# Two first weight sums by accumulating DMA, and a fifth row block pair in seven products, in a two-block transformer kernel

## The chip, the cores and the metric

The kernel runs on one core of one Trainium2 chip. The metric is the device time of one execution in microseconds; the time before is the median of three runs. [...]

## The reference

Two blocks of a transformer, each of two layers, run one after the other on 256 tokens of width 2048, in float32. The change touches one product: the gates of the two layers of the second block (layers 2 and 3 in the kernel's count).

```python
def hybrid_layer(x, norm_w, w_in, ...):
    h = rms_norm_2(x, norm_w)
    proj = h @ w_in                     # (256 x 2048) @ (2048 x 17808)
    (qa, ka, va, za, qi, ki, wi, ub, zb, qc, kc, vc, zc, gates) = jnp.split(proj, ...)
    y_a = (dsa_attention(...) * jax.nn.silu(za)) @ w_a_out
    y_b = (conformer_conv(...) * jax.nn.silu(zb)) @ w_b_out
    y_c = (stick_breaking_attention(...) * jax.nn.silu(zc)) @ w_c_out
    g = jax.nn.sigmoid(gates).reshape(b, s, N_BRANCH, D_MODEL)
    merged = g[:, :, 0] * y_a + g[:, :, 1] * y_b + g[:, :, 2] * y_c
    return x + merged @ w_out
```

The gates are 6144 columns wide: three branches of 2048.

## The kernel before

**Streaming of weights.** Each weight matrix passes once, in fills. A fill is 256 rows of a weight by 512 columns (512 KB), loaded by a DMA that SP issues into one of six buffers `raw`. ACT rounds it to `wh` (step `hi`), DVE computes the rest `wl = raw - wh` (step `lo`), each into one of five buffers (`SPLIT = 5`), and PE multiplies: a product of a 128 x 128 block of the input with a 128 x 512 block of the weight is three matmuls of 512 columns (`wh` with the input's high part, `wl` with the high part, `wh` with its low part). The input has 256 tokens, so 2 blocks of rows, and a fill has 2 blocks of weight rows: 4 products for each fill.

**Seven products for eight.** Two neighbouring gate gemms, a (left 512 columns) and b (right 512 columns), form a duo. A duo has eight row block pairs (256 rows of the weight each), so in the plain way two fills and 8 products for each pair. A pair with a star in the strings `GATES_OF_2` and `GATES_OF_3` is done by the Strassen-Winograd scheme in 7 products, in four fills: `a` (2 products), `b` (2), `x` (2) and `y` (1). With the blocks B11, B21 of a and B12, B22 of b, the sums of weight blocks were: `t_outer`, x = (B12 - B11, B12 - B22), one DVE instruction of 1024 columns into a third buffer; `t_inner`, B22 - x[0]; `t_last`, B21 minus that, 512 columns each. `hi` and `lo` then run on x and y too. The matching sums of the input (`s_sum`, `s_hi`, `s_lo`) are made once in a layer for each starred pair number and serve all gate duos. The products go to six PSUM banks, which `duo_copy`, `duo_middle`, `duo_outer`, `duo_inner` and `duo_end` join. Each layer has five gate duos of this kind (`GATES`), with starred pairs 1, 2, 4, 6; a duo is followed by the two gemms y (1024 rows by 512 columns each) that it gates.

**Buffers of x.** In the gates x has three places beside the six `raw` (`place_raw`): two are made of four of the five `tmp` buffers, one lies in a region of `G`. They are used in turn, and one is free again once `lo` of its x fill is done.

**Order.** All engines run in order. The order is made ahead of time by a planner (`Plan.settle`): it plays all steps through with an estimated duration and gives each engine the step that can start first. The order of pairs in a duo is the string's order. `raw` is issued as soon as its buffer's last reader (`lo`) is done. The gate duos of layer 2 lie at about 1548 to 1850 us, those of layer 3 at 2554 to 2855 us.

Of the kernel before, what the change touches and what calls it, by code (L numbers as in the profile page):

```python
# [12 lines left out]
RAW = 6  # L13
# [3 lines left out]
XS = 3  # L17
# [102 lines left out]
class Lane:  # L120
# [118 lines left out]
    def dma_add(self, dst, src):  # L239
        if self.e is None:  # L240
            self.plan.step.dma = size(dst) * dst.shape[0] * 4
            self.plan.step.late = 2500.0
            return self.sketch(900)
        return self.e.dma_start(dst, src, accum_op=ALU.add)
# [22 lines left out]
class Plan:  # L267
# [16 lines left out]
    def settle(self, urgency):  # L284
# [21 lines left out]
        while self.done < total:  # L306
# [113 lines left out]
class Program:  # L420
# [426 lines left out]
    def sums_at(self, key, q):  # L847

        kind, L = key
        i = SUMS.get(f"{kind}{L}", SUMS.get(kind)).index(q)  # L850
        if kind == "h":
            hi, lo = self.pairs["Y"][L]
            at = (16, 14)[L] + 2 * i
            hi, lo = (x[:, at:at + 2, :].rearrange("p a b -> p (a b)") for x in (hi, lo))
        elif kind == "mem":
            hi, lo = (x[:, 16 + 2 * i:18 + 2 * i, :].rearrange("p a b -> p (a b)") for x in self.pairs["Y"][0])
        elif kind == "out" and L < 2:
            hi, lo = (self.R[:, 1, 1024 * i + 512 * x:1024 * i + 512 * x + 512] for x in range(2))
        elif kind == "out":
            hi, lo = self.pairs["Y"][L]  # L860
            hi, lo = (x[:, 8 + 2 * i:10 + 2 * i, :].rearrange("p a b -> p (a b)") for x in (hi, lo))
        elif key == ("ub", 2) and i == 2 or kind == "gate" and i == 3:
            hi, lo = self.R[:, 0, 4096:4608], self.R[:, 1, 4096:4608]
        elif kind == "gate" and i > 3:
            hi, lo = (self.R[:, 5 - i, 512 * x:512 * x + 512] for x in range(2))
# [5 lines left out]
    def free_sums(self, key):  # L871

        kind, L = key
        if kind == "gate":
            gid = {2: 12, 3: 16}[L]
            return [*self.y_moved(gid),
                    self.v_zb.at(*((L - 2, c) for c in range(0, 8, 2))),
                    *self.y_moved(gid - 1)]
        if kind == "mem":
            return []  # L880
        if key in (("out", 0), ("out", 1)):
            return [self.v_in.at((("y", 3, 2), ("y", 8, 0))[L])]
        if kind == "out":
# [60 lines left out]
    def spare(self, of, c):  # L944
# [277 lines left out]


def sp_program(P, e):
    def load_memt(n):
# [39 lines left out]

    return {"load_memt": load_memt, "load_mem2": load_mem2, "raw": raw, "store": store, "stored": stored}


def pool_program(P, e):
# [297 lines left out]
def act_program(P, e):  # L1567
# [23 lines left out]
    def hi(f):  # L1591
# [5 lines left out]
        role = P.role[f][0] if f in P.role else None  # L1597
        if role in ("b", "x", "y"):
            e.wait_ge(*P.v_tsum.at((f - "abxy".index(role), {"b": 2, "x": 1, "y": 4}[role])))
        if role not in ("x", "y"):  # L1600
# [18 lines left out]
    def s_hi(of, q):  # L1619
        s = P.tmp.buf(("S", of, q)).rearrange("p (n c) -> p n c", n=4)  # L1620
        e.wait_ge(*P.v_ssum.at(*((of, q, i) for i in range(1, 5))))
        for w in P.free_sums(of):
            e.wait_ge(*w)
# [397 lines left out]
def dve_program(P, e):  # L2021
# [18 lines left out]
    def t_outer(f):  # L2040

        a, b, x = (P.slot[f + i] for i in range(3))
        L = P.fills[f][0].L
        if x >= RAW and P.beside[L, x - RAW][0] == f + 2:
            if x == RAW + 2:
                for w in P.y_moved(13 + 4 * (L - 2)):
                    e.wait_ge(*w)
            else:
                for i in range(2 * (x - RAW), 2 * (x - RAW) + 2):
                    P.tmp.take(("beside", L, i), i)  # L2050
                    e.wait_ge(*P.tmp.free(("beside", L, i)))
        e.wait_ge(*P.raw_loaded(f))
        e.wait_ge(*P.raw_loaded(f + 1))
        if P.leaves[f + 2] is not None:
            e.wait_ge(*P.v_lo.at(P.leaves[f + 2]))
        i, j = 2 * a, 2 * b + 1
        s = slice(i, j + 1, j - i) if i < j else slice(i, j - 1 if j else None, j - i)
        b12 = P.raw[b][:, 0, :].unsqueeze(1).broadcast_to([128, 2, 512])
        e.tensor_tensor(P.raw[x], b12, P.raws[:, s, :], ALU.subtract).then_inc(*P.v_tsum.up((f, 1)))

    def t_inner(f):
        a, b, x = (P.raw[P.slot[f + i]] for i in range(3))
        e.wait_ge(*P.v_tsum.at((f, 1)))
        e.tensor_tensor(b[:, 0, :], b[:, 1, :], x[:, 0, :], ALU.subtract).then_inc(*P.v_tsum.up((f, 2)))

    def t_last(f):
        a, b = (P.raw[P.slot[f + i]] for i in range(2))
        e.wait_ge(*P.v_tsum.at((f, 2)))
        e.wait_ge(*P.v_lo.at(f))
        e.tensor_tensor(a[:, 1, :], a[:, 1, :], b[:, 0, :], ALU.subtract).then_inc(*P.v_tsum.up((f, 4)))  # L2070

    def s_sum(of, q):
# [15 lines left out]
        e.wait_ge(*P.v_ssum.at((*key, "a")))  # L2088
        e.tensor_tensor(s[:, 0, :], a[:, 0, 128:256], a[:, 1, 128:256], ALU.add).then_inc(*P.v_ssum.up((*key, 1)))
        e.tensor_tensor(s[:, 1, :], a[:, 0, 128:256], a[:, 0, 0:128], ALU.subtract).then_inc(*P.v_ssum.up((*key, 3)))  # L2090
        e.wait_ge(*P.v_ssum.at((*key, 1)))
        e.tensor_tensor(s[:, 2, :], s[:, 0, :], a[:, 0, 0:128], ALU.subtract).then_inc(*P.v_ssum.up((*key, 2)))
        e.wait_ge(*P.v_ssum.at((*key, 2)))
# [10 lines left out]
    def duo_middle(n):  # L2104
# [21 lines left out]
    def duo_end(g):  # L2126
# [202 lines left out]
    def flip_x(of, c):  # L2329
# [456 lines left out]
def add_steps(P):  # L2786
# [254 lines left out]
    for f, (gm, _) in enumerate(P.fills):  # L3041
# [152 lines left out]
```

## Time and profile before

| | before |
|---|---|
| median of 3 runs | 2986.84 us (2985.16 to 2987.07) |
| the profiled execution, its own time | 2987.06 us |
| its span | 2985.3 us |
| PE busy | 2967.4 us, 99% |
| PE weight load busy | 2479.1 us, 83% |
| DVE busy | 2525.8 us, 85% |
| ACT busy | 2242.2 us, 75% |
| POOL busy | 8.3 us |
| DMA | 570.34 MB, mean 191 GB/s |

The chain of waits gives PE 96% of the span. A matmul of 512 columns is listed with some 388 ns, but these lie over one another, so the listed durations of a group add up to more than the time they take; the time of a matmul on the path is the distance between the starts of two in a row.

### The profile page before, as it was taken

What the parts mean: (1) busy time and instruction counts of PE and PEld (TensorE: products, weight loads), DVE (VectorE), ACT (ScalarE), POOL (GpSimd) and SP (SyncE); (2) the same over time, 40 slices, a digit from 0 to 9 for tenths busy, and PEclk for the clock granted to TensorE, in tenths of its full rate; (3) what the DMA queues carried; (4) which work ended last, traced back from release to release, by engine and by line L of the source; (5) the groups of instructions that cost most, each with busy time, mean ns of one, the idle gap of its engine ahead of it and who ended that gap; (6) DMA issues with size and microseconds to landing.
All of it is one profiled execution on the core that took longest, in us unless ns stands there. A gap on an engine that the chain in (4) does not pass through costs nothing.

```text
span 2985.3 us, 38308 instructions
## 1 busy us (share of the span) xinstructions
PE 2967.4 (99%) x13679; PEld 2479.1 (83%) x13679; DVE 2525.8 (85%) x4023; ACT 2242.2 (75%) x3827; POOL 8.3 (0%) x21
## 2 busy tenths in 40 slices
PE   8999999999999999999999999999999999999998
PEld 7888888877888888888888888888888888888887
DVE  6778679787779899999988888888998998888887
ACT  8797686968877676799885557677778999665684
POOL 0000000000000000000000000000000000000000
PEclk9999999999999999999999999999999999999999
DMA  9656656665556575556565666666565666566565
GB/s 328 191 166 178 179 165 218 205 181 173 177 171 216 170 220 170 177 170 190 177 194 181 202 208 204 205 198 197 154 195 176 182 185 183 177 213 204 181 205 176
DMA packets 305838, 570.34 MB, mean 191 GB/s; under 512 B 18368, under 2 KB 45152, under 8 KB 305264
## 3 DMA queue, kind: packets, MB, share of 16 engines
q1 hardware_dynamic: 301728, 557.65, 59.8%
q10 hardware_dynamic: 3040, 6.42, 0.6%
q0 software_dynamic: 880, 3.83, 0.4%
q8 instruction: 108, 1.77, 0.2%
q14 instruction: 82, 0.67, 0.1%
HBM read 565.73 MB, written 2.10 MB: 190 GB/s over the span
## 4 chain that ended last, share of the span: by engine, by line
PE 96%; DVE 1%; ACT 1%; DMA 1%; issue 0%; DVEq 0%; SPq 0%; ACTq 0%
PE gp L152 83%; PE bk L152 13%; ACT G L167 1%; DVE wl L178 1%; ACT wh L167 0%; DMA raw<-in_w_in 0%; DMA raw<-in_ev_w_mem_kv 0%; DVE merged L231 0%; PE bk L155 0%; DVE merged L178 0%; DVE nat L184 0%; DVE nat L178 0%; DVE merged L184 0%; DVE raw L178 0%; DVE merged L191 0%
## 5 line engine op out<-in xcount | busy, mean ns | idle before, releaser
L167 ACT ACTIVATE wh<-raw 128x1024 fp32r<-128x1024 f32 (+2 forms) x1138 | 1148.6, 1024 | 580.6 <-PE gp L152 459.8
L178 DVE TENSOR_TENSOR wl<-raw,wh 128x1024 fp32r<-128x1024 f32 (+2 forms) x1138 | 1319.5, 1174 | 296.7 <-ACT wh L167 289.7
L152 PE MATMUL gp<-wh,Hh 128*128 128x512 f32 (+3 forms) x2130 | 825.6, 388 | 0.6 <-DVE wl L178 0.5
L152 PE MATMUL gp<-wl,Hh 128*128 128x512 f32 (+3 forms) x2130 | 818.2, 384 | 0.0
L152 PE MATMUL gp<-wh,Hl 128*128 128x512 f32 (+3 forms) x2130 | 818.0, 384 | 0.0
L152 PE MATMUL gp<-wh,Yh 128*128 128x512 f32 (+2 forms) x1676 | 651.3, 389 | 9.2 <-DVE wl L178 9.2
L152 PE MATMUL gp<-wh,Yl 128*128 128x512 f32 (+2 forms) x1676 | 646.6, 386 | 0.0
L152 PE MATMUL gp<-wl,Yh 128*128 128x512 f32 (+2 forms) x1676 | 646.6, 386 | 0.0
L152 PEld LDWEIGHTS gp<-wh,Hh 128*128 128x128 f32 x2130 | 400.2, 188 | 80.7 <-issue 2.2
L152 PEld LDWEIGHTS gp<-wh,Hl 128*128 128x128 f32 x2130 | 400.1, 188 | 78.7
L152 PEld LDWEIGHTS gp<-wl,Hh 128*128 128x128 f32 x2130 | 400.2, 188 | 76.7
L152 PEld LDWEIGHTS gp<-wh,Yh 128*128 128x128 f32 x1676 | 315.5, 188 | 71.8 <-DVE wl L178 10.1
L152 PEld LDWEIGHTS gp<-wh,Yl 128*128 128x128 f32 x1676 | 315.4, 188 | 62.2
L152 PEld LDWEIGHTS gp<-wl,Yh 128*128 128x128 f32 x1676 | 315.6, 188 | 61.1
L167 ACT ACTIVATE G<-nat 32x256 f32<-32x256 f32 (+2 forms) x672 | 264.9, 394 | 11.3 <-DVE nat L231 1.9
L184 DVE SCALAR_TENSOR_TENSOR merged<-merged,cc 128x256 f32<-128x256 f32 x480 | 201.4, 478 | 0.0
L167 ACT ACTIVATE G<-tmp 32x192 f32<-32x192 f32 (+1 forms) x416 | 153.6, 369 | 6.7 <-DVE tmp L231 1.0
L167 ACT ACTIVATE nat<-gp,small 128x512 f32<-128x512 f32 (+3 forms) x178 | 102.6, 621 | 52.3 <-PE gp L152 49.8
L167 ACT ACTIVATE G<-G 32x256 f32<-32x256 f32 (+1 forms) x284 | 117.2, 413 | 4.3 <-DVE G L231 0.3
L152 PE MATMUL bk<-G 128*128 128x128 f32 (+5 forms) x796 | 117.3, 308 | 0.0
L152 PEld LDWEIGHTS bk<-G 128*128 128x128 f32 (+2 forms) x796 | 100.2, 186 | 12.6 <-issue 4.4
L152 PE MATMUL bk<-wh,R 128*128 128x512 f32 x294 | 106.5, 389 | 0.0
(177 smaller groups left out, 2375.9 us busy)
## 6 DMA issues: line engine op xcount, KB each, us to landing
raw<-in_w_in SPq DMA_DIRECT2D x544, 512.0 KB, 4.2
raw<-in_ev_w_in SPq DMA_DIRECT2D x104, 512.0 KB, 4.3
raw<-in_od_w_in SPq DMA_DIRECT2D x80, 512.0 KB, 4.0
raw<-in_w_out SPq DMA_DIRECT2D x64, 512.0 KB, 5.2
raw<-in_ev_w_out SPq DMA_DIRECT2D x40, 512.0 KB, 4.4
raw<-in_od_w_out SPq DMA_DIRECT2D x36, 512.0 KB, 4.6
raw<-in_w_b_out SPq DMA_DIRECT2D x32, 512.0 KB, 4.9
raw<-in_w_a_out SPq DMA_DIRECT2D x32, 512.0 KB, 5.0
```

Source lines behind the costliest of these rows:

```text
L152: return self.e.matmul(out, l, r, start=start, stop=stop)
L167: return self.e.activation(out, in_, func, **kw)
L178: return self.sketch(157 + size(a) * 1.042) if self.e is None else self.e.tensor_tensor(out, a, b, op)
L184: return self.e.scalar_tensor_tensor(out=out, in0=a, scalar=s, in1=b, op0=op0, op1=op1)
```

## The change

Pair 5 gets a star in all ten gate duos of layers 2 and 3 (`GATES_OF_2`, `GATES_OF_3`): five of eight pairs in 7 products. Of the five starred pairs of a duo the second to the fifth in its order (`NTH_BY_DMA`) no longer have `t_outer` on DVE: SP loads B11 and B22 once more, into the two halves of x (`blocks`, two DMAs of 256 KB), and POOL issues two accumulating DMAs that add B12 from HBM to each half (`blocks_add`). For this all sums change their signs: x = (B12 + B11, B12 + B22), and so on, and the signs in `s_sum`, `duo_middle`, `duo_end` and `duo_residual` change with them; the count of instructions there does not. `t_inner` and `hi` of x wait for the accumulating DMAs. `blocks` may be issued five fills ahead (`AHEAD`), waits for its place to be free, in SP's queue, and at its first use for the sums of the input.

Further: `BY_DMA = ((0, 1),)` gives the adding of one of four `merge` steps of branch 0 to two accumulating DMAs on POOL, in each layer. Sums of the input in `out` of layers 0 and 1 lie in another buffer, so two waits (`load_mem2`, `flip_x`) go. The planner's estimate of DMA time changes (400 to 360 bytes a nanosecond, an accumulating one 1.63 times its size), so that it may order steps otherwise anywhere.

```diff
-BY_DMA = ()
+NTH_BY_DMA = (1, 2, 3, 4)
+AHEAD = 5
+BLOCKS_BY_DMA = (("gate", 2), ("gate", 3))
+BY_DMA = ((0, 1),)
...
-GATES_OF_2 = ('0 *1 3 *2 *4 5 *6 7', '0a *1 *2 3b 0b 3a 5 *6 *4 7', ...
+GATES_OF_2 = ('0 *1 3 *2 *4 *5 *6 7', '0a *1 *2 3b 0b 3a *5 *6 *4 7', ...
...
+    def added_up(self, f):
+        d = self.role[f][1]
+        nth = [u for u in d.units if self.role[u][0] == "a"].index(f)
+        return d.sums in BLOCKS_BY_DMA and nth in NTH_BY_DMA and self.slot[f + 2] >= RAW
...
+    def blocks(f):
+
+        (a, j), b, x = P.fills[f], P.fills[f + 1][0], P.slot[f + 2]
+        e.behind("raw", P.loaded_before[f + 1 - AHEAD])
+        room_beside(P, e, f)
+        for h, gm in enumerate((a, b)):
+            k, c = 256 * j + 128 * h, gm.ranges[0][0]
+            e.dma_start(P.raw[x][:, h, :], gm.w[k:k + 128, c:c + 512]).then_inc(*P.s_xload[x - RAW].up((f, h), 16))
...
+    def blocks_add(f):
+
+        b, j = P.fills[f + 1]
+        x, c = P.slot[f + 2], b.ranges[0][0]
+        e.wait_ge(*P.s_xload[x - RAW].at((f, 0), (f, 1)))
+        for h in range(2):
+            e.dma_add(P.raw[x][:, h, :], b.w[256 * j:256 * j + 128, c:c + 512]).then_inc(*P.s_xadd[x - RAW][h].up(f, 16))
...
-        e.tensor_tensor(P.raw[x], b12, P.raws[:, s, :], ALU.subtract).then_inc(*P.v_tsum.up((f, 1)))
+        e.tensor_tensor(P.raw[x], b12, P.raws[:, s, :], ALU.add).then_inc(*P.v_tsum.up((f, 1)))
 
     def t_inner(f):
         a, b, x = (P.raw[P.slot[f + i]] for i in range(3))
-        e.wait_ge(*P.v_tsum.at((f, 1)))
-        e.tensor_tensor(b[:, 0, :], b[:, 1, :], x[:, 0, :], ALU.subtract).then_inc(*P.v_tsum.up((f, 2)))
+        for w in P.first_sums(f, 0):
+            e.wait_ge(*w)
+        if P.added_up(f):
+            e.wait_ge(*P.raw_loaded(f + 1))
+        e.tensor_tensor(b[:, 0, :], b[:, 1, :], x[:, 0, :], ALU.add).then_inc(*P.v_tsum.up((f, 2)))
...
         if role == "a":
-            for s in ("t_outer", "t_inner", "t_last"):
+            if P.added_up(f):
+                add("sp", "blocks", f)
+                add("pool", "blocks_add", f)
+            else:
+                add("dve", "t_outer", f)
+            for s in ("t_inner", "t_last"):
                 add("dve", s, f)
```

How the order moves. SP's queue in layer 2, from the last loads ahead of the first gate duo on. Before:

```order
L237 DMA raw<-in_w_b_out 128x2x512 x4
L237 DMA raw<-in_w_in 128x2x512 x16
L237 DMA raw<-in_w_b_out 128x2x512 x8
L237 DMA raw<-in_w_in 128x2x512 x16
L237 DMA raw<-in_w_a_out 128x2x512 x8
```

The same place now, where `tmp` and `G` are the places of x:

```order
L240 DMA raw<-in_w_b_out 128x2x512 x4
L240 DMA raw<-in_w_in 128x2x512 x6
L240 DMA tmp<-in_w_in 128x512 x2
L240 DMA G<-in_w_in 128x512 x2
L240 DMA raw<-in_w_in 128x2x512 x2
L240 DMA tmp<-in_w_in 128x512 x2
L240 DMA raw<-in_w_in 128x2x512 x4
L240 DMA tmp<-in_w_in 128x512 x2
L240 DMA raw<-in_w_in 128x2x512 x4
L240 DMA raw<-in_w_b_out 128x2x512 x8
```

Between the 16 fills of the first gate duo now stand four pairs of half-size loads. POOL, which had nothing in the gates but constants, gets this there (layer 2, first 22 accumulating DMAs):

```order
L230 MEMSET merged 128x8x30
L247 DMA tmp<-in_w_in 128x512 x2
L247 DMA G<-in_w_in 128x512 x2
L247 DMA tmp<-in_w_in 128x512 x8
L247 DMA G<-in_w_in 128x512 x2
L247 DMA tmp<-in_w_in 128x512 x2
L247 DMA G<-in_w_in 128x512 x2
L247 DMA tmp<-in_w_in 128x512 x2
L247 DMA merged<-nat 128x512 x2
```

Each row of two is one starred pair; the row on `merged` is the merge step. DVE in the first gate duo of layer 2, before:

```order
L178 TENSOR_TENSOR wl3<-raw,wh3 128x1024
L178 TENSOR_TENSOR G<-raw 128x1024
L178 TENSOR_TENSOR wl4<-raw,wh4 128x1024
L178 TENSOR_TENSOR wl0<-raw,wh0 128x1024
L178 TENSOR_TENSOR raw<-raw 128x512
L178 TENSOR_TENSOR wl1<-tmp,wh1 128x1024
L178 TENSOR_TENSOR raw<-raw,G 128x512
L178 TENSOR_TENSOR wl2<-raw,wh2 128x512
```

and now:

```order
L181 TENSOR_TENSOR wl3<-raw,wh3 128x1024
L181 TENSOR_TENSOR raw<-raw,G 128x512
L181 TENSOR_TENSOR wl4<-raw,wh4 128x1024
L181 TENSOR_TENSOR wl0<-raw,wh0 128x1024
L181 TENSOR_TENSOR raw<-raw 128x512
L181 TENSOR_TENSOR wl1<-tmp,wh1 128x1024
L181 TENSOR_TENSOR wl2<-raw,wh2 128x512
L181 TENSOR_TENSOR raw<-raw,tmp 128x512
```

`G<-raw` (`t_outer`) is gone, and `raw<-raw,G` (`t_inner`) stands in its place; it now waits for a DMA, in front of the next `lo`.

## Rows read from the trace of the kernel before

**Rows 1.** The page: span, and busy time of each engine.
```profile
span 2985.3 us, 38308 instructions
PE 2967.4 (99%) x13679; PEld 2479.1 (83%) x13679; DVE 2525.8 (85%) x4023; ACT 2242.2 (75%) x3827; POOL 8.3 (0%) x21
```

**Rows 2.** The chain of waits: shares by engine; two long pieces (start, us, what).
```profile
PE 96%; DVE 1%; ACT 1%; DMA 1%; issue 0%; DVEq 0%; SPq 0%; ACTq 0%
...
918.39 48.96 PE bk L152 x216
...
1474.16 48.99 PE gp L152 x216
```

**Rows 3.** The waits of PE: total, times, longest, in us.
```profile
PE gp L152 <- DVE wl L178: 9.7, 4, 8.5
PE bk L152 <- DVE merged L178: 0.2, 1, 0.2
```

**Rows 4.** Timeline of PE, fifth gate duo of layer 2: start, duration, operation [idle before].
```profile
1836.67 0.39 PE L152 MATMUL bk<-wl,R 128*128 128x512 f32 x1
1836.89 0.39 PE L152 MATMUL bk<-wh,R 128*128 128x512 f32 x1
1837.38 0.50 PE L152 MATMUL gp<-wh,Hh 128*128 128x512 f32 x1
...
1837.96 0.40 PE L152 MATMUL gp<-wh,Hl 128*128 128x512 f32 x1
1838.86 0.50 PE L152 MATMUL gp<-wh,Hh 128*128 128x512 f32 x1 [0.51 <-DVE wl L178]
```

**Rows 5.** Windows in the gates: length, busy time of each engine, clock, DMA share, GB/s.
```profile
1618.00:1622.00 4.00, 4.00 (x19) 3.32 (x18) 2.31 (x2) 1.24 (x2) 0.00 (x0) 1.00 1.01 355
...
1646.00:1650.00 4.00, 4.00 (x19) 3.30 (x19) 3.59 (x4) 2.97 (x3) 0.00 (x0) 1.00 1.03 378
1595.00:1850.00 255.00, 254.40 (x1121) 210.00 (x1121) 220.80 (x218) 155.06 (x185) 0.00 (x0) 1.00 0.62 202
```

**Rows 6.** DVE from 1595 to 1850 us, by form: count, busy, mean ns, idle before.
```profile
L178 DVE TENSOR_TENSOR wl<-raw,wh 128x1024 fp32r<-128x1024 f32 x98 | 118.0, 1220 | 19.8 <-ACT wh L167 18.7
L178 DVE TENSOR_TENSOR tmp<-raw 128x1024 f32<-128x1024 f32 x12 | 14.7, 1223 | 5.5 <-DMA raw<-in_w_in 5.4
...
L178 DVE TENSOR_TENSOR raw<-raw 128x512 f32<-128x512 f32 x16 | 11.0, 687 | 0.4
L178 DVE TENSOR_TENSOR wl<-raw,wh 128x512 fp32r<-128x512 f32 x15 | 10.3, 686 | 2.4 <-ACT wh L167 2.4
...
L178 DVE TENSOR_TENSOR merged<-nat,merged 128x1024 f32<-128x1024 f32 x6 | 7.4, 1226 | 0.2
```

**Rows 7.** ACT in the same stretch, by form.
```profile
L167 ACT ACTIVATE wh<-raw 128x1024 fp32r<-128x1024 f32 x97 | 101.6, 1058 | 73.7 <-PE gp L152 58.3 <-DVE raw L178 12.8 <-PE bk L152 1.7
...
L167 ACT ACTIVATE wh<-raw 128x512 fp32r<-128x512 f32 x16 | 10.1, 629 | 12.1 <-PE gp L152 8.3 <-DVE raw L178 2.7 <-PE bk L152 1.1
```

**Rows 8.** Waits in the same stretch, all engines: total, times, longest.
```profile
ACT wh L167 <- PE gp L152: 73.3, 66, 2.1
...
DVE tmp L178 <- DMA raw<-in_w_in: 5.4, 6, 1.5
```

**Rows 9.** DMA issues: count, KB each, median us from issue to landing.
```profile
raw<-in_ev_w_mem_kv SPq DMA_DIRECT2D x16, 512.0 KB, 8.6
...
raw<-in_w_in SPq DMA_DIRECT2D x32, 256.0 KB, 3.2
...
tab<-in_c_tab POOLq DMA_DIRECT2D x2, 256.0 KB, 4.0
```

**Rows 10.** DMA issues of 1595 to 1850 us alone.
```profile
raw<-in_w_in SPq DMA_DIRECT2D x65, 512.0 KB, 4.8
```

**Rows 11.** Waits of SP's queue over the whole span.
```profile
SPq L237 <- DVE wl L178: 2500.5, 991, 12.2
```

More of the change, by code:

```diff
@@ L241, in dma_add @@
             self.plan.step.dma = size(dst) * dst.shape[0] * 4
-            self.plan.step.late = 2500.0
+            self.plan.step.late, self.plan.step.dma = 2500.0, self.plan.step.dma * 1.63
             return self.sketch(900)
@@ L496, in signals @@
         self.s_raw = [sig(f"s_raw{i}") for i in range(RAW)]
+        self.s_xload = [sig(f"s_xload{i}") for i in range(XS)]
+        self.s_xadd = [[sig(f"s_xadd{i}{h}") for h in range(2)] for i in range(XS)]
         self.s_mem = [sig(f"s_mem_{i}") for i in range(4)]
@@ L831, in by_dve, with first_sums @@
         return BY_DVE and gm.L < 2 and gm.g > 13 and f not in self.role and f % BY_DVE == 0
+    def added_up(self, f):
+        d = self.role[f][1]
+        nth = [u for u in d.units if self.role[u][0] == "a"].index(f)
+        return d.sums in BLOCKS_BY_DMA and nth in NTH_BY_DMA and self.slot[f + 2] >= RAW
+    def first_sums(self, f, *halves):
+        if self.added_up(f):
+            return [self.s_xadd[self.slot[f + 2] - RAW][h].at(f) for h in halves]
+        return [self.v_tsum.at((f, 1))]
     def raw_loaded(self, f):
@@ L857, in sums_at @@
         elif kind == "out" and L < 2:
-            hi, lo = (self.R[:, 1, 1024 * i + 512 * x:1024 * i + 512 * x + 512] for x in range(2))
+            hi, lo = (x[:, 8 + 2 * i:10 + 2 * i, :].rearrange("p a b -> p (a b)") for x in self.pairs["H"][L])
         elif kind == "out":
@@ L864, in sums_at @@
         elif kind == "gate" and i > 3:
-            hi, lo = (self.R[:, 5 - i, 512 * x:512 * x + 512] for x in range(2))
+            hi, lo = (self.R[:, 1, 2048 + 512 * x:2560 + 512 * x] for x in range(2))
         else:
@@ L869, in sums_at, with free_sums @@
         return tuple(x.rearrange("p (n c) -> p n c", n=4) for x in (hi, lo))
[L871 removed]
+    def free_sums(self, key, q):
         kind, L = key
@@ L875, in free_sums @@
             gid = {2: 12, 3: 16}[L]
-            return [*self.y_moved(gid),
+            return [*self.y_moved(gid), *(self.y_moved(gid + 1) if SUMS["gate"].index(q) > 3 else []),
                     self.v_zb.at(*((L - 2, c) for c in range(0, 8, 2))),
@@ L881, in free_sums @@
         if key in (("out", 0), ("out", 1)):
-            return [self.v_in.at((("y", 3, 2), ("y", 8, 0))[L])]
+            return [self.p_mm.at(self.h_end[L].end)]
         if kind == "out":
@@ L1221, in gated, with room_beside @@
         return r[:, :, gr.dh * h:gr.dh * h + gr.dh]
+def room_beside(P, e, f):
+    x, L, d = P.slot[f + 2], P.fills[f][0].L, P.role[f][1]
+    if x >= RAW and P.added_up(f):
+        e.wait_ge(*P.v_s.at(*((d.sums, q) for q in SUMS[d.sums[0]])))
+    if x >= RAW and P.beside[L, x - RAW][0] == f + 2:
+        if x == RAW + 2:
+            for w in P.y_moved(13 + 4 * (L - 2)):
+                e.wait_ge(*w)
+        else:
+            for i in range(2 * (x - RAW), 2 * (x - RAW) + 2):
+                P.tmp.take(("beside", L, i), i)
+                e.wait_ge(*P.tmp.free(("beside", L, i)))
+    if P.leaves[f + 2] is not None:
+        e.wait_ge(*P.v_lo.at(P.leaves[f + 2]))
 def sp_program(P, e):
@@ L1264, in stored @@
         e.wait_ge(*P.s_out[n].at("o"))
-    return {"load_memt": load_memt, "load_mem2": load_mem2, "raw": raw, "store": store, "stored": stored}
+    return {"load_memt": load_memt, "load_mem2": load_mem2, "raw": raw, "blocks": blocks, "store": store, "stored": stored}
 def pool_program(P, e):
@@ L1597, in hi @@
         role = P.role[f][0] if f in P.role else None
-        if role in ("b", "x", "y"):
-            e.wait_ge(*P.v_tsum.at((f - "abxy".index(role), {"b": 2, "x": 1, "y": 4}[role])))
+        if role == "x":
+            for w in P.first_sums(f - 2, 0, 1):
+                e.wait_ge(*w)
+        if role in ("b", "y"):
+            e.wait_ge(*P.v_tsum.at((f - "abxy".index(role), {"b": 2, "y": 4}[role])))
         if role not in ("x", "y"):
@@ L1621, in s_hi @@
         e.wait_ge(*P.v_ssum.at(*((of, q, i) for i in range(1, 5))))
-        for w in P.free_sums(of):
+        for w in P.free_sums(of, q):
             e.wait_ge(*w)
@@ L2042, in t_outer @@
         a, b, x = (P.slot[f + i] for i in range(3))
[L2043 to L2051, printed above, removed]
+        room_beside(P, e, f)
         e.wait_ge(*P.raw_loaded(f))
         e.wait_ge(*P.raw_loaded(f + 1))
-        if P.leaves[f + 2] is not None:
-            e.wait_ge(*P.v_lo.at(P.leaves[f + 2]))
         i, j = 2 * a, 2 * b + 1
@@ L2069, in t_last @@
         e.wait_ge(*P.v_lo.at(f))
-        e.tensor_tensor(a[:, 1, :], a[:, 1, :], b[:, 0, :], ALU.subtract).then_inc(*P.v_tsum.up((f, 4)))
+        e.tensor_tensor(a[:, 1, :], a[:, 1, :], b[:, 0, :], ALU.add).then_inc(*P.v_tsum.up((f, 4)))
     def s_sum(of, q):
@@ L2078, in s_sum @@
         e.wait_ge(*P.v_in.at(P.lhs(gm, 2 * q)))
-        for w in P.free_sums(of):
+        for w in P.free_sums(of, q):
             e.wait_ge(*w)
@@ L2088, in s_sum @@
         e.wait_ge(*P.v_ssum.at((*key, "a")))
[L2089 to L2090 removed]
+        e.tensor_tensor(s[:, 0, :], a[:, 1, 128:256], a[:, 0, 128:256], ALU.subtract).then_inc(*P.v_ssum.up((*key, 1)))
+        e.tensor_tensor(s[:, 1, :], a[:, 0, 0:128], a[:, 0, 128:256], ALU.subtract).then_inc(*P.v_ssum.up((*key, 3)))
         e.wait_ge(*P.v_ssum.at((*key, 1)))
[L2092 removed]
+        e.tensor_tensor(s[:, 2, :], s[:, 0, :], a[:, 0, 0:128], ALU.add).then_inc(*P.v_ssum.up((*key, 2)))
         e.wait_ge(*P.v_ssum.at((*key, 2)))
@@ L2108, in duo_middle @@
         e.wait_ge(*P.p_mm.at(d.last["6"][0]))
-        e.tensor_tensor(T[:, 3, :], P.banks_of(d)["6"], T[:, 0, :], ALU.add).then_inc(*v.up((n, "v1")))
+        e.tensor_tensor(T[:, 3, :], T[:, 0, :], P.banks_of(d)["6"], ALU.subtract).then_inc(*v.up((n, "v1")))
         P.bank.give(("duo", n, "6"), v, (n, "v1"))
@@ L2132, in duo_end @@
         b = P.nat.buf(g)
-        e.tensor_tensor(b, b, P.gp[g % 2][:, :, :], ALU.add).then_inc(*P.v_duo.up((n, "c" + x)))
+        e.tensor_tensor(b, P.gp[g % 2][:, :, :], b, ALU.add if x == "a" else ALU.subtract).then_inc(*P.v_duo.up((n, "c" + x)))
     def duo_residual(g):
@@ L2143, in duo_residual @@
         x = P.X[:, :, 512 * gm.part:512 * gm.part + 512]
-        e.tensor_tensor(x, P.nat.buf(g), x, ALU.add).then_inc(*P.v_duo.up((gm.duo.n, g)))
+        e.tensor_tensor(x, x, P.nat.buf(g), ALU.add if gm is gm.duo.a else ALU.subtract).then_inc(*P.v_duo.up((gm.duo.n, g)))
     def in_lo(of, i):
@@ L2340, in flip_x @@
             e.wait_ge(*P.p_mm.at(P.last_sums(("gate", 2))))
-        if of == ("x", 2) and P.outs[1][0].duo:
-            e.wait_ge(*P.p_mm.at(P.last_sums(("out", 1))))
         if c >= 2:
```

14 lines of the change are left out of this document (7 added, 7 removed).

## The prediction, on record before the changed kernel ran

> **What bounds the kernel now.** I read the page first: PE is busy 2967.4 of 2985.3 us [rows 1]. The chain of waits says the same, PE 96% [rows 2], and PE's own waits come to 9.9 us in the whole run, 8.5 of it a single one [rows 3]. So PE's instructions, not their supply, set the time, and the first question is what one matmul costs there. The groups list 388 to 390 ns, but they overlap: the chain has 216 matmuls in 48.99 us and 216 in 48.96 us [rows 2], and two starts in a row lie 0.22 us apart in the timeline [rows 4]. That is 48.99 / 216 = 0.2268 us for a matmul and 0.680 us for a product of three. [...]
>
> In the gates PE is busy 254.40 of 255 us; DVE has 220.80, ACT 155.06, the DMA engines a share of 0.62 at 202 GB/s [rows 5]. ACT stands 73.3 us, in 66 waits, because PE has not yet freed a `wh` buffer [rows 8]: the supply is ahead by all of its five buffers about half of the time. It is not always: in the fifth duo PE waits twice for `wl`, where starts lie 0.49 and 0.90 us apart instead of 0.23 [rows 4], together some 0.9 us.
>
> **The change, part by part.**
>
> **Products.** Ten pairs go from 8 to 7 products: ten products, 30 matmuls. The order confirms it: PE's program has 13215 instructions before and 13185 now, and all other shapes keep their counts. 30 x 0.2268 = **6.80 us** less, all on the path, since PE is the path. That is 0.23%: no more than this can come from the star on pair 5.
>
> **DVE.** 30 of 40 `t_outer` in the gates go (10 remain, one for each duo) and two merges: 30 x 1.223 + 2 x 1.226 = 39.1 us [rows 6]. The ten new stars bring a `lo` of x (1.220), a `lo` of y (0.686), `t_inner` and `t_last` (0.687 each): 32.8 us. Two more sets of input sums, six instructions each of at most 512 columns, are at most 12 x 0.69 = 8.3 us. Net between -6.3 and +2.0 us of 2525.8 us: nothing. What matters is the place. A starred pair by DMA takes DVE 3 x 1.220 + 0.686 + 2 x 0.687 = 5.72 us and PE 7 x 0.680 = 4.76 us. Four in a row, as in the first duo (`*2 *4 *5 *6`), leave DVE 22.9 - 19.0 = 3.9 us behind. Before, `*2 *4` with `t_outer` (6.94 us each) left it 13.9 - 9.5 = 4.4 us behind and then came an unstarred pair (2.44 against 5.44 us). The cover of split buffers bore that, so I cost it at nothing.
>
> **ACT.** 10 x (1.058 + 0.629) = 16.9 us more [rows 7], hidden under its 73.3 us of waiting for PE in one layer's gates alone.
>
> **DMA.** This is the real price. A gate duo loads 16 x 512 KB = 8.39 MB in 60 products (40.8 us): 206 GB/s. Now 4 x 1 MB come on top, half of them accumulating: 12.58 MB in 59 products (40.1 us), 314 GB/s. In four starred pairs in a row it is 2.10 MB in 4.76 us, 441 GB/s, and the most that the rows show is 355 to 378 GB/s, at a share of 1.01 to 1.03 [rows 5]. The 8.39 MB of such a run take 22.2 to 23.6 us against PE's 19.0: 3.2 to 4.6 us that have to be fetched ahead. SP's queue waits for free buffers 2500 of 2985 us [rows 11], so the six `raw` are nearly always filled ahead; the y gemms after a duo (32 products, 21.8 us, 4.19 MB) bring the mean down to 16.8 MB in 61.9 us, 271 GB/s, and each duo starts afresh. What an accumulate adds to its bytes no row shows; zero at the least, and at the most as much again for reading its target, 2.1 MB or 5.6 to 5.9 us more for a run of four.
>
> **The new wait.** `t_inner` waits for load and accumulate of x, and behind it on DVE stand all later `lo`, then PE. A 256 KB load from SP lands after 3.2 us, a 256 KB one from POOL after 4.0 [rows 9]: 7.2 us in all for a lone chain. With full queues: the 512 KB loads of the run's start took 8.6 us [rows 9], those in the gates 4.8 [rows 10]; I take 4.8 + 8.6 = 13.4 us as the upper end. The time there is: x has three places, so the fourth in a row may load once `lo` of the x three stars back is done, two whole pairs plus part of one before it is needed, 10 to 12 us. I take 9 to 10 us, nearest to the row of the gates (4.8 us, twice): it just fits. At 13.4 us the last pairs of a run come some 2 us late, and five split buffers, half of the time full, stand against that. `blocks` can also hold up SP: the loads behind it wait while its place is not free.
>
> [...]
>
> **Merge by DMA, the moved sums, the two waits gone, the planner's numbers.** The merge's result is read one branch later, at least a duo (61.9 us) away: nothing. The released waits stood on SP and DVE where PE shows no idle time [rows 3]: nothing. A different order elsewhere can neither win nor lose much where PE never waits; bound 1 us each way, from the 0.9 us in the fifth duo.
>
> **Sum.** The profiled execution took 2987.06 us, 1.76 over its span and 0.22 over the median. 2987.06 - 6.80 = 2980.26; against the median 2986.84 it is 2980.04. I add 0.5 us for new short waits, half of the 0.9 us that one such place costs now: **2980.5 us**.
>
> **Rivals.**
>
> **B, partly eaten.** In some of the ten duos, those with four stars in a row, x lands late and PE stands 1 to 2 us. For it: the 10 to 12 us against 9 to 10, and DVE already waits for plain loads in 6 places, 5.4 us, before `t_outer` [rows 8]. Against it: PE did not notice those. Five such duos at 1 to 2 us: 5 to 10 us back, 2985 to 2990; with fewer 2981 to 2985. A change that falls within 0.2% (5.97 us, about what a measurement of this kernel can tell from no change) is mostly this.
>
> **C, slower.** The accumulates cost as much again in the DMA engines, so that a run of four takes 28 to 29.5 us against 19.0, and each duo ends in a wait of `t_inner` for its last x, which no fetching ahead covers (buffers hold some 5 to 8 us). Each duo saves 0.68 us; a stall over that makes the kernel slower, one over 0.68 + 0.60 = 1.28 us slower by over 0.2%. At 2 us for each it is 2980.0 + 20 = 3000 us. For it: 441 against 378 GB/s without any overhead. Against it: the mean of a duo is 271 GB/s.
>
> [...]
>
> **E, more than the products.** The waits of the fifth duos go too, because DVE has no `t_outer` there: 2 x 0.9 us, 2978.2 us.
>
> **How the numbers follow.** Forecast (0 to 0.9 us of new waits, 2979.5 to 2980.9) 0.38; E 0.08; B 0.30; C 0.18; D 0.06. The limit of faster by over 0.2% is 2980.87 us, so close above the forecast that noise of the median moves a part of it across: faster 0.40 (forecast and E, less some, plus the best of B), within 0.2% 0.36 (most of B, a part of C), slower 0.24. The range takes in E and B and the mild half of C: 2978.0 to 2994.0; the forecast's own is 2979 to 2982.
>
> **What would show it.** Right: 30 fewer matmuls, PE starts 0.227 us apart through the gates, `t_inner` (`raw<-raw,tmp`, `raw<-raw,G`) waiting for DMA at most 1 us at a time, share of DMA in the gates about 0.83 (271 GB/s, where 202 make a share of 0.62 [rows 5]). [...] If all gates are clean and the time is still above 2982, my price of a matmul is wrong.

## The result, and the profile after

The changed kernel takes 3090.29 us (median of 6 runs, 3088.07 to 3092.7) where the kernel before takes 2986.99 (6 runs): a ratio of 1.0346, 95% interval 1.0335 to 1.0357. It is 103 us slower; forecast were 6.5 us less, with a range up to 2994. Time and sign were both wrong.

The page of the changed kernel; the first two lines answer to [rows 1], the last is the chain by engine, which answers to [rows 2]:

```profile
span 3086.3 us, 38549 instructions
...
PE 2991.0 (97%) x13649; PEld 2490.7 (81%) x13649; DVE 2524.0 (82%) x4043; ACT 2256.7 (73%) x3849; POOL 80.8 (3%) x105
...
PE 80%; issue 8%; DMA 5%; DVE 4%; ACT 1%; POOL 1%; SPq 0%; DVEq 0%; ACTq 0%
```

PE has its 30 matmuls less (13649 for 13679), and DVE's busy time is what it was (2524.0 for 2525.8), as forecast. But the chain is PE for 80% only, and 8% are "issue": time in which an engine on the chain waited for nothing that the profile shows. PE's waits (us in total, times, longest), which were 9.9 us [rows 3]:

```profile
PE bk L155 <- DVE wl L181: 65.4, 22, 9.4
PE gp L155 <- DVE nat L187: 11.9, 2, 6.3
PE gp L155 <- DVE wl L181: 9.1, 2, 8.8
PE gp L155 <- DVE merged L187: 0.9, 1, 0.9
PE bk L155 <- DVE merged L181: 0.2, 1, 0.2
```

They make 87.5 us, 77.6 more than before. The other 23.4 of the 101.0 us of span are PE's longer busy time (23.6 us), of which more below. The two waits for `nat` come from the same place: DVE's step on `nat` stood behind a `t_inner` that waited 7.30 and 6.66 us. The waits of DVE for the accumulating DMAs, which no row of before has:

```profile
DVE raw L181 <- DMA tmp<-in_w_in: 58.3, 13, 8.5
DVE raw L181 <- DMA G<-in_w_in: 42.0, 8, 12.6
```

These are `t_inner`: 100.3 us in 21 waits. ACT's `hi` of x waits for the same DMAs, 26.1 us in 8. Why the DMAs come late stands in the timeline of POOL, from the first accumulating DMA of layer 2 on (start, duration, operation, idle time before and what ended it):

```profile
1568.95 0.90 POOL L247 DMA_DIRECT2D tmp<-in_w_in  x1 [601.28 <-DMA tmp<-in_w_in]
1574.45 0.86 POOL L247 DMA_DIRECT2D tmp<-in_w_in  x1 [4.60 <-issue]
1579.42 0.86 POOL L247 DMA_DIRECT2D G<-in_w_in  x1 [4.11 <-issue]
1584.43 0.84 POOL L247 DMA_DIRECT2D G<-in_w_in  x1 [4.15 <-issue]
1589.15 0.86 POOL L247 DMA_DIRECT2D tmp<-in_w_in  x1 [3.88 <-issue]
```

POOL is busy 0.86 us with each, but starts them 4.7 to 5.5 us apart, and what ends its idle time is "issue". The second DMA of a pair (1574.45) has no wait of the program in front of it at all. The landing takes about as long as the spacing:

```profile
tmp<-in_w_in POOLq DMA_DIRECT2D x54, 256.0 KB, 5.1
G<-in_w_in POOLq DMA_DIRECT2D x26, 256.0 KB, 4.6
```

So each accumulating DMA seems to start when the one before has landed. The view of their line, L247, has the whole run: what ended the idle time before them (us, times), and the landing:

```profile
  issue: 361.0, 72
DMA to landing us min/median/max: 3.8/4.9/8.8
```

At the median landing, eight in a gate duo are 8 x 4.9 = 39 us of POOL's queue for 40.1 us of products, and 9.8 us for each starred pair that PE wants every 4.76 us. By the 72 waits a turn is longer, 361.0 / 72 + 0.86 = 5.9 us in the mean, and eight are 47 us. A place in layer 2, POOL, DVE and PE:

```profile
1746.06 0.88 POOL L247 DMA_DIRECT2D G<-in_w_in  x1 [3.83 <-issue]
```

```profile
1750.18 0.69 DVE L181 TENSOR_TENSOR raw<-raw,G 128x512 f32<-128x512 f32 x1 [7.69 <-DMA G<-in_w_in]
```

```profile
1745.11 0.39 PE L155 MATMUL gp<-wh,Hl 128*128 128x512 f32 x1
1752.07 0.79 PE L155 MATMUL bk<-wh,R 128*128 128x512 f32 x1 [6.57 <-DVE wl L181]
1752.66 0.63 PE L155 MATMUL bk<-wl,R 128*128 128x512 f32 x1
1753.09 0.63 PE L155 MATMUL bk<-wh,R 128*128 128x512 f32 x1
```

DVE stands 7.69 us, PE 6.57. And after the stall matmuls start 0.43 us apart instead of 0.227. The windows show why (columns as in [rows 5]): the granted clock is 0.50 after PE had been idle. In the gates PE has 12 waits of 3.0 us or more, and in a window of 2 us soon after each of them the granted clock is 0.50 or 0.51. The length of the wait alone does not settle it below that: it stayed 1.00 after one of 2.81 us (PE starts again at 1827.21) and fell to 0.50 after one of 1.79 (1872.86).

```profile
1752.00:1754.00 2.00, 1.93 (x5) 1.55 (x6) 2.00 (x4) 0.00 (x0) 0.00 (x0) 0.50 0.94 130
...
1560.00:1920.00 360.00, 323.13 (x1353) 262.40 (x1352) 268.16 (x275) 198.60 (x238) 37.34 (x44) 0.94 0.80 232
```

Each long wait is thus paid again in part. PE's busy time rises by 23.6 us though 6.8 us of matmuls are gone.

The longest waits of the gates stand elsewhere, in layer 3, and behind the merge step. Its two accumulating DMAs go through the same queue, ahead of the adds for the next starred pair:

```profile
2786.09 0.86 POOL L247 DMA_DIRECT2D merged<-nat  x1 [4.08 <-issue]
2795.22 0.86 POOL L247 DMA_DIRECT2D merged<-nat  x1 [8.27 <-issue]
2799.30 0.87 POOL L247 DMA_DIRECT2D G<-in_w_in  x1 [3.22 <-issue]
```

```profile
2803.46 0.69 DVE L181 TENSOR_TENSOR raw<-raw,G 128x512 f32<-128x512 f32 x1 [12.64 <-DMA G<-in_w_in]
2805.34 0.79 PE L155 MATMUL bk<-wh,R 128*128 128x512 f32 x1 [9.43 <-DVE wl L181]
```

The two take 13.2 us of the queue there (2786.09 to 2799.30).

### The profile page after: what moved, and what is told of

It reads as the page before. It is cut to its first block, busy times and chain, and to the rows that moved or that the text cites. A ratio compares the mean times of both kernels' runs of the same rounds, so it can differ in the third digit from the quotient of the medians.

```text
span 3086.3 us, 38549 instructions
## 1 busy us (share of the span) xinstructions
PE 2991.0 (97%) x13649; PEld 2490.7 (81%) x13649; DVE 2524.0 (82%) x4043; ACT 2256.7 (73%) x3849; POOL 80.8 (3%) x105
## 2 busy tenths in 40 slices
DMA packets 329457, 613.36 MB, mean 199 GB/s; under 512 B 20992, under 2 KB 47776, under 8 KB 328880
## 3 DMA queue, kind: packets, MB, share of 16 engines
q0 software_dynamic: 12976, 25.85, 5.0%
## 4 chain that ended last, share of the span: by engine, by line
PE 80%; issue 8%; DMA 5%; DVE 4%; ACT 1%; POOL 1%; SPq 0%; DVEq 0%; ACTq 0%
PE gp L155 69%; PE bk L155 10%; DMA tmp<-in_w_in 3%; DVE wl L181 2%; DMA G<-in_w_in 1%; ACT G L170 1%; POOL tmp L247 1%; DVE nat L181 1%; ACT wh L170 0%; POOL G L247 0%; DVE raw L181 0%; SPq L240 0%; DVE tmp L181 0%; DMA raw<-in_ev_w_mem_kv 0%; DVE merged L187 0%
## 5 line engine op out<-in xcount | busy, mean ns | idle before, releaser
L155 PE MATMUL gp<-wh,Yh 128*128 128x512 f32 (+3 forms) x1646 | 640.4, 389 | 10.0 <-DVE wl L181 9.1
L155 PE MATMUL gp<-wl,Yh 128*128 128x512 f32 (+3 forms) x1646 | 635.7, 386 | 0.0
L155 PE MATMUL gp<-wh,Yl 128*128 128x512 f32 (+3 forms) x1646 | 635.7, 386 | 0.0
L155 PEld LDWEIGHTS gp<-wh,Yh 128*128 128x128 f32 x1646 | 309.9, 188 | 71.2 <-DVE wl L181 10.2
L170 ACT ACTIVATE G<-nat 32x256 f32<-32x256 f32 (+2 forms) x672 | 264.9, 394 | 10.7 <-DVE nat L234 1.0
L155 PE MATMUL bk<-wh,R 128*128 128x512 f32 x324 | 129.5, 427 | 57.8 <-DVE wl L181 57.8
L155 PEld LDWEIGHTS bk<-wh,R 128*128 128x128 f32 x324 | 67.1, 207 | 80.1 <-DVE wl L181 65.9
```

Of the source, the lines that this page charges most:

```text
L155: return self.e.matmul(out, l, r, start=start, stop=stop)
L170: return self.e.activation(out, in_, func, **kw)
```

## The experiments

Two theories stood at the start. **Ring**: the kernel sets a buffer of fixed size, `dynamic_dma_scratch_size=512`. The theory takes it for a ring of the descriptors (the orders for the single transfers) of POOL's DMAs, with room for one accumulating DMA of 128x512; the next waits until it has been moved. **Rivals**: accumulating DMAs of one queue run one by one whatever the ring (order); or the DMA engines are simply full (load, the forecast's rival C); or the star itself does it.

**m_ring512** and **m_ring16384**: a program of its own with nothing else in it (N is 8).

```diff
...
+            for i in range(N):
+                e.dma_start(big[:, i, :], w[128 * i:128 * i + 128, 0:512], accum_op=ALU.add).then_inc(s_a, 16)
+            e.wait_ge(s_a, 16 * N)
+            for i in range(N):
+                e.dma_start(big[:, N + i, :], w[128 * i:128 * i + 128, 512:1024]).then_inc(s_b, 16)
+            e.wait_ge(s_b, 16 * N)
+            for i in range(N):
+                e.dma_start(big[0:64, 2 * N + i, :], w[128 * i:128 * i + 64, 512:1024], accum_op=ALU.add).then_inc(s_c, 16)
```

> A small kernel of its own, which computes nothing of the reference: POOL issues eight accumulating DMAs of 128x512 from HBM, then eight plain ones of 128x512, then eight accumulating ones of 64x512, one behind the other to places of their own, with the descriptor ring of 512 bytes that both kernels have; nothing else runs. Theory ring (the ring holds the descriptors of one such DMA, so the next is issued only when the one before has been moved): accumulating 128x512 start 4 to 5 us apart as in the changed kernel (4.5 to 5.0 us there), plain ones the same or a little less (3 to 4 us), the 64x512 ones, with half the descriptors, two or more in flight: 1 to 3 us apart. Rival load (the spacing comes from full DMA queues beside it): without other traffic all start about 0.9 us apart, the time that POOL is busy for one.

> The same small kernel with a descriptor ring of 16384 bytes. Theory ring: all three kinds start about 0.9 us apart (POOL's own 0.86 us). Rival order (accumulating DMAs of one queue run one after the other whatever the ring): accumulating ones stay 4 to 5 us apart, plain ones about 0.9 us.

POOL with 512 bytes (L31 accumulating 128x512, L34 plain 128x512, L37 accumulating 64x512):

```profile
18.25 1.02 POOL L31 DMA_DIRECT2D big<-in_w  x1 [17.81 <-DVEq L13]
22.95 0.90 POOL L31 DMA_DIRECT2D big<-in_w  x1 [3.67 <-issue]
27.24 0.88 POOL L31 DMA_DIRECT2D big<-in_w  x1 [3.39 <-issue]
...
53.25 1.68 POOL L34 DMA_DIRECT2D big<-in_w  x3 [3.53 <-DMA big<-in_w]
58.52 1.59 POOL L34 DMA_DIRECT2D big<-in_w  x3 [3.58 <-issue]
...
68.01 2.57 POOL L37 DMA_DIRECT2D big<-in_w  x3 [3.28 <-DMA big<-in_w]
```

and with 16384:

```profile
18.25 7.29 POOL L31 DMA_DIRECT2D big<-in_w  x8 [17.81 <-DVEq L13]
33.51 4.31 POOL L34 DMA_DIRECT2D big<-in_w  x8 [7.97 <-DMA big<-in_w]
43.67 6.67 POOL L37 DMA_DIRECT2D big<-in_w  x8 [5.85 <-DMA big<-in_w]
```

With 512 bytes one accumulating 128x512 goes at a time, 4.3 us apart with no other traffic, and three plain or three half-size ones; with 16384 all eight go one behind the other. In this program neither order nor load makes the spacing. The plain ones were more in flight than the expectation had it. The eight accumulating ones also show their price in the DMA engines when nothing holds them back. Each group starts when the one before has landed, so eight take 33.51 - 18.25 = 15.3 us, against 10.2 us for eight plain ones (33.51 to 43.67).

**ring768**: the changed kernel with a larger ring; an unused tensor makes the room.

```diff
-        sb("pad", [128, 16])
...
-    nc = _bacc.Bacc("TRN2", target_bir_lowering=False, num_devices=1, dynamic_dma_scratch_size=512)
+    nc = _bacc.Bacc("TRN2", target_bir_lowering=False, num_devices=1, dynamic_dma_scratch_size=768)
```

> The changed kernel with a ring of 768 instead of 512 bytes (an unused pad of 64 bytes goes to make room). Theory ring: two accumulating DMAs fit at once, the pair of a starred block starts about 1 us apart, a pair costs POOL some 5.8 instead of 9.8 us, and most of the 103 us go: 2980 to 3010 us. Rival order, or rival load (the DMA engines are full): nothing changes, 3085 to 3095 us.

Measured 2999.42 us (ratio to before 1.0043, 1.0028 to 1.0058): 91 of the 103 us are gone with 256 bytes. POOL at the same place, two at once:

```profile
1568.72 1.79 POOL L247 DMA_DIRECT2D tmp<-in_w_in  x2 [601.87 <-DMA tmp<-in_w_in]
1573.72 0.84 POOL L247 DMA_DIRECT2D G<-in_w_in  x1 [3.21 <-issue]
1575.27 0.85 POOL L247 DMA_DIRECT2D G<-in_w_in  x1 [0.71 <-issue]
```

**serial768**: ring768 with POOL told to wait for each landing.

```diff
             e.dma_add(P.raw[x][:, h, :], b.w[256 * j:256 * j + 128, c:c + 512]).then_inc(*P.s_xadd[x - RAW][h].up(f, 16))
+            e.wait_ge(*P.s_xadd[x - RAW][h].at(f))
```

> The kernel with the ring of 768 bytes (2999.4 us) with one thing added: after each accumulating DMA POOL waits for its landing before it starts the next. Theory ring (the loss of the changed kernel is that each accumulating DMA waits for the one before): it goes back to the time with 512 bytes, 3080 to 3100 us. Rival (a larger ring helps in some other way, as by faster descriptor writing): it stays within 10 us of 2999.

Measured 3091.75 us (ratio 1.0346, 1.0331 to 1.0362): the changed kernel's ratio, with the large ring. Running them one by one is enough to make the loss, with any effect of a larger ring beside that kept; and ring768 shows that without it 91 us go. This is the cause.

**m_ring576**: the small program with 576 bytes.

```diff
-SCRATCH = 512
+SCRATCH = 576
```

> [...] With 512 one accumulating 128x512 was in flight, three plain ones, three accumulating 64x512. [...] Rival order: one accumulating at a time, whatever the ring; the run with 16384 bytes speaks against it already.

```profile
18.24 1.94 POOL L31 DMA_DIRECT2D big<-in_w  x2 [17.80 <-DVEq L13]
24.83 0.88 POOL L31 DMA_DIRECT2D big<-in_w  x1 [4.65 <-issue]
...
45.74 1.66 POOL L34 DMA_DIRECT2D big<-in_w  x3 [4.49 <-DMA big<-in_w]
```

The accumulating 128x512 start as 2, 1, 1, 2 and 2 at once, where 512 bytes let them start one at a time; plain ones stay at three. The rival order, one accumulating at a time whatever the ring, is not what the trace has. So the number of accumulating ones in flight grows with the ring, but how the ring is counted stays open.

**star_only**: all weight sums on DVE again, the fifth star kept.

```diff
-NTH_BY_DMA = (1, 2, 3, 4)
+NTH_BY_DMA = ()
```

> The changed kernel with all first sums of weight blocks on DVE again (no accumulating DMA for them; pair 5 keeps its star, the merge stays on DMA). Theory ring, and every theory that puts the loss on the accumulating DMAs: the loss goes; DVE has 5 x 6.94 + 3 x 2.44 = 42.0 us of work in a gate duo against PE's 40.1 us, which the y gemms after it can take up, so 2980 to 2990 us. A rival that puts the loss on the star itself or on the moved input sums: 3050 us or more.

Measured 2994.04 us (ratio 1.0024, 1.0015 to 1.0034): outside what I expected, and slower than before. PE waits for `wl` where DVE falls behind:

```profile
PE bk L155 <- DVE wl L181: 9.8, 14, 1.1
```

14 waits of at most 1.1 us: none in two of the ten duos, seven in the last duos of the two layers together, and the first matmul after such a wait is slower too: at 1604.28, after 0.76 us, it is listed with 0.50 us where others have 0.39, and the next starts 0.34 us after it. Against 2980.0 without new waits this version loses 14 us, twice what the star saves. It still has the merge on DMA, the moved sums and the planner's new numbers, so that not all of the 14 us need be the star's.

**adds_only**: the reverse, four stars as before, the second to fourth by accumulating DMA, ring 512.

```diff
-NTH_BY_DMA = (1, 2, 3, 4)
+NTH_BY_DMA = (1, 2, 3)
...
-GATES_OF_2 = ('0 *1 3 *2 *4 *5 *6 7', ...
+GATES_OF_2 = ('0 *1 3 *2 *4 5 *6 7', ...
```

> The changed kernel without the star on pair 5: four starred pairs as before, of which the second to fourth get their first sums by accumulating DMA; ring 512. Theory ring: 6 accumulating DMAs of 4.9 us are 29.4 us of POOL in a gate duo of 40.8 us, more than PE's time where starred pairs stand in a row; still clearly slower than before, 3010 to 3050 us. Rival (the loss needs the fifth star: DVE or DMA engines too full only with it): 2987 to 2995 us.

Measured 3002.53 us (ratio 1.0054, 1.0039 to 1.0069), below my range, though a turn was longer than the 4.9 us taken: 239.2 us of "issue" in 46 waits, 6.1 us in the mean with POOL's 0.86. Six are 36 us in 40.8. The longest wait of DVE, 10.7 us, stands behind the two DMAs of a merge here too. This version and star_only lose 16 and 7 us against the kernel before, both together 103 (with one more pair of adds in each duo, 47 us of queue for 40.1).

**narrow**: ring 512, accumulating DMAs of a quarter of the columns; the other three quarters of the sums are left out.

```diff
-                e.dma_add(P.raw[x][:, h, :], b.w[256 * j:256 * j + 128, c:c + 512])
+                e.dma_add(P.raw[x][:, h, 0:128], b.w[256 * j:256 * j + 128, c:c + 128])
```

> The changed kernel, ring 512, with accumulating DMAs of 128 instead of 512 columns: as many rows and descriptors, a quarter of the bytes (three quarters of each block are not added, so the gates are not those of the reference). Theory ring: spacing falls only by the time of moving the bytes (from 4.9 us to perhaps 3.5 to 4.2), so much of the loss stays, 3020 to 3070 us. Rival load (bytes in full DMA engines): 31 MB less through them, most of the loss goes, 2985 to 3010 us.

Measured 3018.65 us (ratio 1.0105, 1.009 to 1.012), 72 us less, 1 us outside the range of the ring theory and well outside that of load. They still go one at a time:

```profile
1570.12 0.90 POOL L247 DMA_DIRECT2D tmp<-in_w_in  x1 [601.94 <-DMA tmp<-in_w_in]
1574.22 0.86 POOL L247 DMA_DIRECT2D tmp<-in_w_in  x1 [3.20 <-issue]
1577.15 0.86 POOL L247 DMA_DIRECT2D G<-in_w_in  x1 [2.06 <-issue]
```

with 2.9 to 5.4 us from start to start at this place. Over the run the idle time that ends in "issue" is 266.5 us in 68 waits, so that a turn is 4.8 us in the mean instead of 5.9, and eight are 38 us instead of 47, now less than the duo's 40.1. The page counts 15.7 MB less (597.64 for 613.36), not the 31 of the expectation, in as many packets of POOL's queue (12976 in both). The ring makes the turns; bytes lengthen each of them, and with three quarters of the bytes 72 of the 103 us went.

**planned**: ring 512, the planner told of POOL's 4.9 us.

```diff
-            return self.sketch(900)
+            return self.sketch(4900)
...
-                moment = dma_free + 700.0 + s.late if s.dma else t + extra + when
+                moment = dma_free + 700.0 + s.late + when - s.ups[0][2] if s.dma else t + extra + when
```

> The changed kernel, ring 512, with the planner told that POOL is busy 4.9 us with each accumulating DMA and the second lands 4.9 us after the first. Nothing else changes but the order of steps. Theory ring: the order can hide part, but the adds of a duo still need 39 us of POOL where x is wanted every 4.8 us: 3040 to 3090 us. Rival (the loss comes from DVE being made to wait at a badly chosen place in its order, and better places would do): under 3000 us.

Measured 3088.83 us (ratio 1.0346, 1.0331 to 1.0362). The order did change, and DVE's waits for the accumulating DMAs fell from 100.3 to 54.5 us while ACT's rose from 26.1 to 56.9, but the time stayed: a planner that knows of the queue found no way around it. That no order at all could is not shown.

**two_adds_768**, and two tries at a better version, **tuned_three_768** and **tuned_two_768**: ring 768 (by the two lines of ring768, not shown again), fewer pairs by DMA, then also another order of pairs.

```diff
-NTH_BY_DMA = (1, 2, 3, 4)
+NTH_BY_DMA = (2, 4)
```

```diff
-NTH_BY_DMA = (1, 2, 3, 4)
+NTH_BY_DMA = (2, 3, 4)
...
-GATES_OF_2 = ('0 *1 3 *2 *4 *5 *6 7', '0a *1 *2 3b 0b 3a *5 *6 *4 7', ...
+GATES_OF_2 = ('0 *1 *5 3 *2 *4 *6 7', '0a *1 *2 *4 0b 3a *5 *6 3b 7', ...
...
-                dma_free = max(dma_free, t + 1300.0) + s.dma / 360.0
+                dma_free = max(dma_free, t + 1300.0) + s.dma / 326.000000
```

The first diff is that of two_adds_768, the second of tuned_three_768, which moves pairs in four duos (not in six, as its expectation says). tuned_two_768 keeps `(2, 4)` and moves pairs in seven duos. Both tuned ones also have the planner's DMA rate of 326 and 1500 ns of POOL for an accumulating DMA.

> The changed kernel, five stars, ring 768, but only the third and fifth starred pair of a duo by accumulating DMA. What is left of the loss at ring 768 (2999.4 us against 2980.0 without any new wait) is, by the theory that the DMA engines are then the bound (share 0.87 from 1560 to 1860 us), mostly gone: 4 MB a layer and duo fewer double reads, DVE at 39.6 us in a duo against 40.1 us: 2982 to 2988 us. By the theory that the latency of the chain load, add, sum is the bound, 2990 to 2996 us.

> A try at a better version: ring 768, five stars, the third to fifth starred pair by accumulating DMA, the planner's rate of DMA set to 326 bytes a nanosecond (202 GB/s at a share of 0.62, as the trace of before has it) and 1500 ns of POOL for an accumulating DMA, and the order of pairs in six of ten duos changed. If an order that spreads the starred pairs takes away the waits that the DMA engines' fullness leaves, 2980 to 2988 us; if a fifth star costs DVE and DMA more than the 6.8 us it saves whatever the order, 2988 to 2996 us.

> The same with the third and fifth starred pair by accumulating DMA, with its own order of pairs. Against 2993.5 us of the version with this choice and the changed kernel's own order: 2982 to 2988 us if the order mattered, 2990 to 2996 us if not.

Measured 2993.5 us (ratio 1.0023, 1.0013 to 1.0034), 2989.94 (1.0012, 1.0002 to 1.0022) and 2990.4 (1.0012, 1.0002 to 1.0021). The first lies in the range of "latency of the chain", not in that of "full DMA engines"; its PE waits are for `wl` (10 waits, 7.4 us), much as in star_only, so I read it as DVE and ACT, not as either; no run shows that. The tuned ones win 3 to 4 us over it, by order and planner's numbers together, and none beats the kernel before.

What is left at ring 768, 2999.42 against 2980.0, has three waits of DVE's `t_inner` in it:

```profile
DVE raw L181 <- DMA raw<-in_w_in: 33.3, 17, 4.9
DVE raw L181 <- DMA G<-in_w_in: 8.5, 3, 5.1
DVE raw L181 <- DMA tmp<-in_w_in: 3.0, 2, 2.5
```

Now the plain loads of B22 are mostly the late ones: from 1560 to 1860 us a `raw` lands after 6.8 us, in the median, where it was 4.8 [rows 10]. That fits the bandwidth the forecast feared (a DMA share of 0.87 there, at 258 GB/s). But the ring of 768 bytes still holds POOL at times, 65.1 us of "issue" in 21 waits, and no run of the whole kernel has a larger one. How the 19 us split between DMA engines, ring and the five stars themselves (14 us in star_only) the runs do not say.

## Why the prediction was wrong

**Right**: the price of a matmul (0.2268 us; 30 fewer), PE as the path, DVE's and ACT's totals. Its sign of being right, `t_inner` waiting at most 1 us at a time, failed: the longest wait is 12.64 us.

**The step that failed is "The new wait"**: "A 256 KB load from SP lands after 3.2 us, a 256 KB one from POOL after 4.0 [rows 9]: 7.2 us in all for a lone chain", and then "I take 9 to 10 us". The latencies were about right (4.5 to 4.6 us for the load, 4.6 to 5.1 for the add). What was missing is that a starred pair has two accumulating DMAs and that they, and those of the pairs before, go one at a time. `t_inner` waits for the first of its pair, behind all earlier ones; `hi` of x waits for both, some 4.6 + 4.9 + 4.9 = 14.4 us for a lone pair. And the queue's throughput, 9.8 us for each pair (11.8 at the mean turn of 5.9) against 4.76, is a bound by itself. The prediction computed throughput for PE, DVE, ACT and the DMA engines, and only latency for POOL's queue.

**The merge by DMA, put at "nothing"**, failed by the same step: its result is indeed read late, but its two DMAs take turns in the queue, and the longest waits of DVE (12.64 us) and of PE in the gates (9.43) stand behind them. What the four such DMAs cost among the adds no run shows.

The kernel before could have told it. The three constants that POOL loads in a row stand in its timeline:

```profile
69.10 0.83 POOL L237 DMA_DIRECT2D masks<-in_c_masks  x1 [67.55 <-DMA X<-in_x]
69.93 0.56 POOL L237 DMA_DIRECT2D tab<-in_c_tab  x1
73.89 0.54 POOL L237 DMA_DIRECT2D small<-in_od_sinks  x1 [3.40 <-issue]
```

Two go at once, the third, 8 KB, waits 3.40 us for "issue" with no wait of the program before it. That this was the full ring, ring768 shows, where the third follows the second without idle time:

```profile
65.22 0.57 POOL L240 DMA_DIRECT2D tab<-in_c_tab  x1
65.77 0.54 POOL L240 DMA_DIRECT2D small<-in_od_sinks  x1
```

84 DMAs times about 4 us would have been some 330 us of one queue in twice 300 us of gates, an estimate from those rows. The name of the size stands in the kernel's last function.

**Rival C** had the sign and a similar place (a wait of `t_inner` that fetching ahead cannot cover) with another cause; its chance was 0.18 and its price 20 us, a fifth of what came. The price of an accumulate lay inside the prediction's bounds, half as much again (15.3 against 10.2 us for eight), and the DMA share was 0.80 from 1560 to 1920 us, not near 1. C held a stall of 2 us a duo; the measured loss is near 10 (103 us over some ten duos, the clock's part in it), I think because the deficit adds up over four pairs in a row (4 x (9.8 - 4.76) = 20 us, an estimate, half of it covered). **Rival D** (chance 0.06), that POOL's DMAs come late because DVE's work holds POOL up, is not seen: POOL's own time for such a DMA is 0.86 us in the gates and 0.89 us in the small program with DVE idle.

**The 0.5 us "for new short waits"** was too small even without the queue, and that lay hidden under the first error. No version with five stars came nearer to 2980.0 than 2989.9 us (tuned_three_768); star_only, with more work on DVE than the forecast had, lost 14 us, and ring768, with the forecast's share of work, 19. DVE's sum for the pairs, "I cost it at nothing", left out the steps that join the banks of a duo: `duo_middle` and `duo_inner` of 512 columns, `duo_outer` and two `duo_end` of 1024, 5.0 us beside PE's 40.1. How much of the 10 to 19 us is DVE's the runs do not say.

**The clock**: the forecast took one price, 0.2268 us, for every matmul. The granted clock fell to 0.50 after each wait of 3.0 us or more in the gates (mean 0.987 over the run), and PE's busy time grew by 23.6 us where it should have fallen by 6.8: some 30 of the 103 us.

## What to carry to other kernels

An engine's queue can have a throughput of its own that its busy time does not show (here 0.86 us busy in a turn of 5.9): before work is moved to POOL's DMAs, look for two of them in a row in the trace and read the distance of their starts, and what ends the idle time between. "issue" in front of an instruction without a wait of the program can be a full resource, and the ring of 512 bytes was one here: 256 bytes more of it were worth 91 us. A step that is itself in no hurry, as the merge, still takes its turns in a queue that others wait for (13.2 us at 2786.09). And where PE is the bound at 99%, a saving of one product needs the supply behind it counted at that place, not over the run, since here each stall of 3.0 us or more was also paid in the clock, which was 0.50 after it.

## What the runs showed of the hardware that was not expected

A ring of 512 bytes (`dynamic_dma_scratch_size`) took one accumulating DMA of 128x512 float32, or three of 64x512, or three plain ones of 128x512, at a time (m_ring512); 576 bytes took two accumulating ones at times (m_ring576), 768 two (ring768), 16384 at least eight (m_ring16384). Accumulating from HBM took the engines longer than copying: eight of 256 KB in 15.3 us against 10.2 us for eight plain ones, from the first start until the next group could start, with nothing else on the core. After a wait of 6.57 us PE's matmuls started 0.43 us apart, twice the 0.227 of before, at a granted clock of 0.50.
